# Attention outputs waited for tile by tile, and a layer's last weight buffer handed back inside the next norm's transposes

## The reference

```python
# layer 0 ("even")
x = x + concat(swa_sink_attention(q, k, v), s5_mixer(u)) @ even_w_out   # 8 heads of 64, and a state-space half
x = x + (silu(hn @ w_gate[0]) * (hn @ w_up[0])) @ w_down[0]             # "ffn0", hidden width 2816
# layer 1 ("odd")
x = x + stick_breaking_attention(q, k, v) @ odd_w_out                   # 16 heads of 64
x = x + (silu(hn @ w_gate[1]) * (hn @ w_up[1])) @ w_down[1]             # "ffn1"
# second block
merged = sigmoid(z_g) * (o_g @ w_proj_gla) + sigmoid(z_m) * (o_m @ w_proj_moba)
x = x + merged @ w_out              # o_g: gated linear attention, o_m: block attention ("moba"), 8 heads of 64
x = x + memory_attention(...) @ w_co                                    # "c", 4 heads of 128
x = x + hier_moe(...)               # router, top 2 of 8 experts in one of 4 groups; 32 experts of width 512
return rmsnorm(x)
```

## Time and profile before

| | us |
|---|---|
| median of 3 runs | 1400.45 (1399.97 to 1400.62) |
| the profiled execution | 1398.65 |
| its span, first to last instruction | 1396.5 |
| PE busy | 1186.7 (85% of the span) |
| PEld busy | 928.5 (66%) |
| DVE busy | 676.8 (48%) |
| ACT busy | 469.3 (34%) |
| mean granted TensorE clock | 0.934 of full |

### The profile page before, as it was taken

One profiled execution on the slowest core, in us unless ns is written; L12 is line 12 of the kernel. 1 busy time (PEld: TensorE's weight loads), 2 busy tenths in 40 slices (PEclk: granted clock), 3 DMA queues, 4 the chain that ended last, 5 costly groups with the idle time before them and its releaser, 6 DMA issues.

```text
span 1396.5 us, 19896 instructions
## 1 busy us (share of the span) xinstructions
PE 1186.7 (85%) x8160; PEld 928.5 (66%) x8160; DVE 676.8 (48%) x960; ACT 469.3 (34%) x599; POOL 27.0 (2%) x82
## 2 busy tenths in 40 slices
PE   6999999999999999999998999999674666756665
PEld 5886999998987999998896888884221221212121
DVE  7997475556778575556344857552110110101012
ACT  5555343334665443334344534441010100101001
POOL 2310000000000000000000000000000000000000
PEclk9989999999999999999996999999888988888788
DMA  9523365555434365556452345797999999999995
GB/s 255 120 57 121 107 220 190 189 187 180 144 120 144 112 221 191 188 184 208 139 176 66 121 151 181 314 367 325 421 421 422 422 422 421 422 422 421 423 420 220
DMA packets 137016, 343.41 MB, mean 246 GB/s; under 512 B 9818, under 2 KB 99036, under 8 KB 112372
## 3 DMA queue, kind: packets, MB, share of 16 engines
q1 hardware_dynamic: 135292, 337.96, 64.7%
q0 software_dynamic: 1552, 4.47, 1.8%
q10 hardware_dynamic: 104, 0.02, 0.0%
HBM read 339.80 MB, written 2.62 MB: 245 GB/s over the span
## 4 chain that ended last, share of the span: by engine, by line
PE 60%; DMA 23%; DVE 10%; ACT 3%; issue 3%; SPq 2%; POOL 0%; DVEq 0%; ACTq 0%; POOLq 0%
PE ps L1285 16%; PE ps L1287 15%; PE ps L1286 15%; DMA ring<-in_w_exp_down_dram 11%; DMA ring<-in_w_exp_up_dram 11%; PE ps L1764 4%; PE ps L1739 3%; SPq L526 1%; DVE piece_lo L1939 1%; ACT piece_hi L774 1%; PE ps L1161 1%; DMA MT<-in_ssm_b_im_dram 1%; PE ps L1389 1%; PE ps L1539 1%; PE ps L1685 1%
## 5 line engine op out<-in xcount | busy, mean ns | idle before, releaser
L1285 PE MATMUL ps<-HT_hi,piece_hi 128*128 128x256 f32 x1088 | 311.2, 286 | 7.2 <-DVE HT_lo L1930 4.3
L1286 PE MATMUL ps<-HT_lo,piece_hi 128*128 128x256 f32 x1088 | 308.9, 284 | 0.0
L1287 PE MATMUL ps<-HT_hi,piece_lo 128*128 128x256 f32 x1088 | 308.8, 284 | 0.0
L1939 DVE TENSOR_TENSOR piece_lo<-ring,piece_hi 128x2048 fp32r<-128x2048 f32 x118 | 266.9, 2286 | 83.8 <-ACT piece_hi L774 83.2
L774 ACT ACTIVATE piece_hi<-ring 128x2048 fp32r<-128x2048 f32 x118 | 223.0, 1912 | 196.1 <-PE ps L1287 161.3
L1285 PEld LDWEIGHTS ps<-HT_hi,piece_hi 128*128 128x128 f32 x1088 | 209.8, 193 | 10.8 <-issue 7.8
L1739 PE MATMUL ps<-ring,arena 128*32 128x512 f32 x992 | 139.8, 716 | 87.6 <-DMA ring<-in_w_exp_up_dram 67.6
L1286 PEld LDWEIGHTS ps<-HT_lo,piece_hi 128*128 128x128 f32 x1088 | 209.9, 193 | 0.9
L1287 PEld LDWEIGHTS ps<-HT_hi,piece_lo 128*128 128x128 f32 x1088 | 209.8, 193 | 0.0
L1739 PEld LDWEIGHTS ps<-ring,arena 128*32 128x32 f32 x992 | 38.9, 128 | 182.0 <-issue 181.5
L1764 PE MATMUL ps<-ring,arena 128*32 128x512 f32 x464 | 78.9, 799 | 51.3 <-DMA ring<-in_w_exp_down_dram 51.3
(11 more groups left out here) (449 smaller groups left out, 1737.6 us busy)
## 6 DMA issues: line engine op xcount, KB each, us to landing
ring<-in_w_exp_gate_dram SPq DMA_DIRECT2D x64, 1024.0 KB, 18.6
ring<-in_w_exp_up_dram SPq DMA_DIRECT2D x60, 1024.0 KB, 17.6
ring<-in_w_exp_down_dram SPq DMA_DIRECT2D x58, 1024.0 KB, 16.4
ring<-in_ffn_w_gate_dram SPq DMA_DIRECT2D x22, 1024.0 KB, 5.7
ring<-in_ffn_w_up_dram SPq DMA_DIRECT2D x22, 1024.0 KB, 5.4
ring<-in_ffn_w_down_dram SPq DMA_DIRECT2D x22, 1024.0 KB, 7.3
ring<-in_w_in_dram SPq DMA_DIRECT2D x20, 1024.0 KB, 5.4
ring<-in_odd_w_in_dram SPq DMA_DIRECT2D x12, 1024.0 KB, 5.2
```

Source lines behind the costliest of these rows:

```text
L1285: pe.matmul(out, sh, mh, start=start, stop=False, skip_group_check=True)
L1286: pe.matmul(out, sh, ml, start=False, stop=False, skip_group_check=True)
L1287: return pe.matmul(out, sl, mh, start=False, stop=stop, skip_group_check=True)
L1939: ve.tensor_tensor(piece_lo[k % RING][:, :], ring[:, k % RING, :], piece_hi[:, h % HI_SLABS, :].bitcast(F32), ALU.subtract).then_inc(split, 1)
```

## The change

Three edits on PE's instruction stream; no other engine's instructions change.

First, `output_done` no longer stands ahead of norms 1, 2, 3, 4 and 7. `norm` gets an argument `closes` and calls it after its fourth transpose, the one that fills bank 0. Norm 5, after `mix_out`, is left as it was. Second, the output projections of the odd layer and of the memory attention wait for tile i of the attention output ahead of their i-th piece, where they waited for both tiles ahead of the first. Third, in the mixer the wait for `moba_o` stands ahead of `proj_m`, and that for `g_oT` ahead of `proj_g`, behind the last two z projections.

```diff
-            def norm(n, wait=True):
+            def norm(n, wait=True, closes=None):
...
                     if tb == kt % 2 == 1:
                         ins.then_inc(bank_full, 1)
+                        if closes and kt == 1:
+                            output_done(closes)
...
-            def output_part_split(name, pieces, first, opening, closing, hi, lo, ready=None):
+            def output_part_split(name, pieces, first, opening, closing, hi, lo, ready=None, tiles=None):
 
                 for n, i in enumerate(pieces, first):
+                    if tiles is not None:
+                        wait_emptied(pe, tiles, n - first)
...
                 down((count - 1) % 2, 3 * count - 1, base + count, stop=True)
-                pe.wait_ge(mix_full, 4 * (RESIDUAL_NO[name] + 1))
-                pe.nop().then_inc(piece_used, 1)
...
-            output_done("even_out")
-            norm(1, wait=False)
+            norm(1, wait=False, closes="even_out")
             glu(0)
-            norm(2, wait=False)
+            norm(2, wait=False, closes="ffn0")
...
-                wait_all_emptied(pe, name + "_o")
-            output_part_split("odd_out", range(2, 4), 2, 0, 3, MT_hi, odd_lo_of)
-            output_done("odd_out")
-            norm(3, wait=False)
+                if half == 0:
+                    wait_all_emptied(pe, name + "_o")
+            output_part_split("odd_out", range(2, 4), 2, 0, 3, MT_hi, odd_lo_of, tiles="sb1_o")
+            norm(3, wait=False, closes="odd_out")
             glu(1)
-            norm(4, wait=False)
+            norm(4, wait=False, closes="ffn1")
...
             weighted_values("moba", PT2, lambda h, kb: m_v[:, kb, 64 * h:64 * h + 64])
-            wait_all_emptied(pe, "moba_o")
             pe.wait_ge(gla_out, 1)
...
                 ins.then_inc(bank_full, 1)
+            feature_major_split("z", 2, first=6)
             wait_all_emptied(pe, "g_oT")
-            feature_major_split("z", 2, first=6)
             projection_split("proj_g", MT_hi[:, 0:4, :], mixer_lo[:, 0:4, :])
+            wait_all_emptied(pe, "moba_o")
             projection_split("proj_m", MT_hi[:, 4:8, :], mixer_lo[:, 4:8, :])
...
-            wait_all_emptied(pe, "c_o")
-            output_part_split("c_out", range(2), 0, 0, 1, MT_hi, lambda kt: c_lo[:, kt, :])
-            output_done("c_out")
-            norm(7, wait=False)
+            output_part_split("c_out", range(2), 0, 0, 1, MT_hi, lambda kt: c_lo[:, kt, :], tiles="c_o")
+            norm(7, wait=False, closes="c_out")
```

## The result

| | before | after |
|---|---|---|
| median of the runs measured together | 1400.21 us (4 runs, 1397.86 to 1400.62) | 1390.62 us (4 runs, 1390.53 to 1391.92) |
| the profiled execution | 1398.65 | 1390.68 |
| its span | 1396.5 | 1388.9 |
| mean granted TensorE clock | 0.934 | 0.932 |

The ratio is 0.9937, with a 95% interval of 0.9920 to 0.9954: 6.4 to 11.2 us faster, against 8.55 forecast.

What follows compares the result with a forecast made beforehand. PE was taken to bound the dense layers and the DMA stream the experts. 3.2 + 2.7 + 1.3 + 1.15 + 0.2 = 8.55 us off the median 1400.45 gave 1391.9 us, range 1389.2 to 1396.6.

Steps and rivals of the forecast that it cites:

- What PE gains ahead of the stream reaches the end: Full expert load stream, from 952.62 us: time PE gains ahead of it moves the kernel's end by as much.
- the stream absorbs it: Rival: the expert stream starts when it did and the gain becomes a wait for expert weights; 1400.5 us, chance 0.05.
- The mixer's waits: Mixer, ahead of the z projections: both PE gaps go and z starts 3.2 us sooner.
- The clock in the mixer: Mixer's z matmuls: the low 1.2 GHz clock cost 2.7 us, counted as gained.
- with both gaps gone the clock stays up: Mixer: without PE's gaps of 1.53 and 1.69 us the clock does not fall, worth 2.7 us.
- the rule of the Trainium skill: Supports the rival that the mixer's clock falls anyway, after one long idle gap: 5.85 us gain, 1394.6 us, chance 0.17.
- The mixer gives its part back: Rival: z ends sooner but `proj_g` or `proj_m` waits for split pieces; 1397.8 us, chance 0.08.
- The odd output: Odd layer's output projection: PE starts after the first tile instead of the second, 1.3 us sooner.
- the memory output: Memory attention's output projection: PE starts after the first tile, 1.15 us sooner.
- The norms: Norms 1, 2, 3, 4 and 7 with moved hand-backs: 0.2 us at norm 1, nothing counted at the others.
- The late hand-back is covered: Ring loads behind the norms: hand-back 0.6 us later, hidden by 15 us of cover; rival slower, 1420 us, chance 0.03.
- The sum: Whole kernel: terms total 8.55 us, giving a predicted median of 1391.9 us, chance 0.60.

Runs made afterwards that it cites:

- E5: The kernel before with only the mixer's wait for `moba_o` moved, to ahead of `proj_m`; 1395.61 us, ratio 0.9971.
- E6: The kernel before with only the mixer's wait for `g_oT` moved behind the last two z projections; 1395.26 us, ratio 0.9970.
- E4: The kernel before, mixer waits in place, with 12 and 14 unused transposes added ahead of them to keep PE busy; 1397.30 us, ratio 0.9988.
- E9: The changed kernel unaltered, measured again on another occasion; 1392.37 us, ratio 0.9948 to the kernel before.
- E3: The kernel before with only the hand-backs (`output_done`) moved into norms 1, 2, 3, 4 and 7; 1399.16 us, ratio 0.9996.
- E7: The changed kernel with `output_done` of `even_out` and `odd_out` put off into the next feed-forward layer's first projection; 1392.47 us, ratio 0.9943 to before.
- E2: The kernel before with only the tile-by-tile waits of the odd and memory output projections; 1395.26 us, ratio 0.9969.
- E8: The changed kernel with three more edits: norm 7's copies before its second squaring, `mix_out`'s hand-back into norm 5, `sb0_o`'s wait later; 1389.56 us.
- E10: The changed kernel with ACT copying norm 7's two banks ahead of squaring the second half of X; 1389.84 us, ratio 0.9932 to before.

## Why the prediction was right, point by point

- *What PE gains ahead of the stream reaches the end.* Shown in all 14 profiles: from the load to the end of the span 443.9 to 444.5 us, however soon the load came. The rival that the stream absorbs it is out.
- *The mixer's waits, 3.2 us.* Turns to z went from 8.61 to 5.29: 3.32. By halves 1.55 (E5) and 1.93 (E6). Those sum to 0.16 more, and the wait for the bank of moba's first tile, which the prediction had named, is the likely reason: with both gaps gone z starts 1.02 us behind the start of the eight transposes (801.41 to 802.43), just behind DVE's first subtraction, and in E6, where that tile is long done, 0.82 (803.57 to 804.39).
- *The clock in the mixer, 2.7 us.* z's matmuls, from the first start to the last, went from 14.10 to 11.47: 2.63. z to `proj_g` went from 14.68 to 12.15: 2.53, because the pause ahead of `proj_g` is 0.1 us longer where the wait now stands; E4, with the waits left in, has 2.64. The step "with both gaps gone the clock stays up" holds in eight profiles of eight. What the prediction did not see is that one gap gone is enough (E5, E6), though its own comparison, one gap at the odd attention and a full clock, pointed there. By the rule of the Trainium skill that I had set against it (TensorE: Matmul & The Clock Gate, "HAM oscillation — how this bites in real kernels"), it is one long unbroken gap that brings the clock down. The traces don't agree: two gaps of 1.53 and 1.69 us did it, with eight transposes between them, and behind 34 such transposes in a row z ran at 1.00 (E4).
- *The mixer gives its part back.* As a rival it is out, but 0.1 us of it is real for each moved wait: the step to `proj_m`'s first matmul is 0.69 us wherever `moba_o`'s wait stands there and 0.58 in before. I had counted nothing. The rest of the 0.3 us in `proj_g` to `proj_m` (11.84 in before, 12.14 in after) comes and goes with the same code: E9 is after's kernel and has 11.95, and E3, without the edit, 12.08.
- *The odd output, 1.3, and the memory output, 1.15.* 1.37 (313.63 to 312.26) and 1.21 (38.52 to 37.31).
- *The norms, 0.2 at norm 1 and nothing elsewhere.* E3 shows no difference on the whole, and the timelines show each norm. At norm 1, from the first of DVE's four adds to ACT's first copy it took 2.59 us before (137.18 to 139.77) and 2.40 after (137.78 to 140.18), 0.19 us. Over all profiles it is 2.59 to 2.78 in the six kernels without the moved hand-back and 2.40 or 2.41 in the eight with it: the gain is 0.2 to 0.4, and what is left is paced by DVE's adds. From the last matmul ahead of norms 2, 3 and 4 to ACT's first copy it is 1.65, 1.51 and 1.65 us in all fourteen, to 0.01 us: nothing gained. At norm 7 the wait went to ACT's copy, as written.
- *The late hand-back is covered.* E7 hides ten times the delay at two of the five places, E3 the delay itself at all five.
- *The sum, 8.55.* The stages that the edits touch give 3.32 + 2.53 + 1.37 + 1.21 + 0.19 - 0.30 = 8.3 us. The two profiled executions differ by 7.97, since untouched stages scatter both ways (router to expert 0.47 shorter in after; start-up 0.41 and `proj_m` to norm 6 0.36 longer). The medians say 9.6 with the first four runs, 6.7 with E9 and its neighbours, 7.5 over all. The predicted 1391.9 and the 1391.92 over nine runs agree more closely than this allows one to claim: a median of five runs moves by a microsecond or two with the start-up and the clock.
- *The profiled execution lies below the median.* I took its 1.8 us as a constant of the kernel. It was the draw of one execution: that of after lay at 1390.68, on its median of 1390.62.

## What to carry to other kernels

Wait for a tile at its reader, not at the end of its producer, and look at what stands between the two: where independent matmuls can take the place, the whole wait goes. A short idle gap of PE can cost more than itself when a second one is near; closing either of them, or filling both with useless transposes of the right length, kept the clock up here, and such a pair is worth looking for ahead of a long run of matmuls. When terms of a microsecond are at stake, compare stage by stage between fixed points of the trace, because medians of this kernel scatter by more than the term.

## What was not expected of the hardware

- The cost of the mixer's low clock varies with the program unchanged up to there but for 1.3 us of time: z to `proj_g` 14.68 and 14.72, but 13.54 in E2.
- Behind the router's 32 matmuls of 36 columns the clock fell to the 1.2 GHz level in some profiles with PE busy from the router's first matmul on: in after it was busy for 2.50 of 2.50 us from 930 to 932.5 at 1.00, and as busy in the next window at 0.50. Ahead of them PE had idled 0.98 us, but so it had in E9 (0.99), where the clock stayed at 1.00 with the same matmuls, as it did in E8 and E10. Where it falls goes with 12.5 to 14.9 us for the stretch to the first expert matmul; I found nothing in the program that settles it.
- The stretch from norm 4 to moba's turns took 151.0 to 153.9 us with the same instructions, at a granted clock between 0.60 and 0.79 for the 20 us windows within 740 to 780 us. That is as large as any single term of this change.
